# Opening stage of an encoder block regrouped by feature block, with keys, values and first queries accumulated together

## The chip, the core and the metric

The kernel runs on one NeuronCore of a Trainium2 chip. The metric is the device time of one execution in microseconds (us). Before the change it is 852.07 us, the median of 3 runs (851.49 to 852.62). One further execution was taken with the hardware profiler; every duration below comes from that one.

## What is computed

One layer of a bidirectional encoder on x (512 tokens, 1024 features, fp32). Cut to what matters here:

```python
mod = silu(c) @ w_ada + b_ada                 # (6 * 1024): shift1, scale1, gate1, shift2, scale2, gate2
h = rms_norm(x, norm1_gain) * (1 + scale1) + shift1
cb, cc, cu, q, k, v, ga, gb = split(h @ w_in) # 3x1024, 1024, 256, 256, 2x1024 columns
y_a = cb * dwconv3(cc * cu)
y_b = windowed_gqa(rms_norm(q), rms_norm(k), v, sink)   # 16 query heads, 4 key heads of 64
x = x + gate1 * ((sigmoid(ga) * y_a + sigmoid(gb) * y_b) @ w_o)
x = x + gate2 * conv_ffn(rms_norm(x) * (1 + scale2) + shift2)
```

## The kernel before

The program is written engine by engine, every wait by hand. A 128-feature slice of the 1024 features is a **block**; there are KT = 8. Each product of fp32 values is split: a value is rounded to a high part in fp32r (ScalarE, function `high`, line 480) and the rest is its low part (GpSimd, function `low`, line 404), and a product is three matmuls, high x high, high x low, low x high (`three`, lines 728 to 730). A **unit** is 128 output columns of a weight matrix times the 512 tokens: 8 blocks x 3 matmuls of 512 columns. Weights come as pairs of units (256 columns, 1 MB) through two slots `w_raw`.

The opening makes h and from it keys, values and the first queries:

- SyncE (SP) issues all loads in one queue: c, x (4 x 512 KB), the first two sixths of w_ada (shift1 and scale1) as 16 chunks of 512 KB, each the 128 rows of one k and 512 of the 1024 columns of both parts (line 342), small parameters after the fourth, and the key and value weights (line 314).
- VectorE (DVE) multiplies each chunk by silu(c) of its 128 rows and adds it to `acc0` (`gemv0`, line 1092), 1024 elements a partition at a time; chunk 8 is multiplied by TensorE instead (line 752). After chunks 0 to 7 the sum for blocks 0 to 3 is complete, after 8 to 15 that for blocks 4 to 7. Each half is transposed by TensorE (line 761), reduced (line 1099) and made into a shift `mod` and a factor `amp` (lines 1105, 1106).
- GpSimd (POOL) multiplies the transposed x by its row factors (`hT`, line 422). ScalarE (ACT) makes the high part of h (line 516), DVE its float value (line 1118), DVE or POOL its low part `h_lo` (lines 1123, 427).
- TensorE (PE) makes keys and values token by token, `token_major`, lines 728 to 730 with 256 columns: keys for blocks 0 to 3, values in part, then blocks 4 to 7. Only behind it stand the two query units, 48 matmuls of 512 columns. Keys are normalised on DVE (1144 to 1147), transposed (803), and split (534, 1163).

After the opening come, for each of the 4 groups g of heads, 10 or 12 units (kinds C, U, B, A, Q, G) in **slots** of half a unit (12 matmuls), between which the attention of the group stands at slots given by tables (`SCORE`, `TURN`, `Q0_TURN`). The first unit of group 0 (C) needs `q_st`, the split queries (line 1175). Then follow the output projection and the channel-mixing layer.

```python
for n in range(KT):
    gemv0(n)
mods(0)
```

are DVE's lines for the first half of the modulation; `mods(0)` waits for PE's `mod_turn(0)`.

## Time and profile before

| what | value |
|---|---|
| median of 3 runs | 852.07 us (851.49 to 852.62) |
| profiled execution, its own time | 850.04 us |
| its span, first to last instruction | 848.24 us |
| mean granted TensorE clock | 0.974 of full |
| PE busy | 793.4 us (94%) |
| DVE, ACT, POOL busy | 551.9, 366.7, 370.4 us |
| data read | 93.43 MB |

A span is read from its first instruction at 0. Durations of pipelined matmuls overlap: the distance between two starts is what one costs, the printed duration is longer. "Idle before" is the time in which the engine had nothing to do, with what ended it behind the arrow.

### The profile page before, as it was taken

To read this page: it belongs to the slowest core of one execution; us is meant where nothing else is said; L and a number is where in the kernel's file an instruction comes from. 1 tells how busy PE (TensorE), PEld (TensorE's weight loads), DVE (VectorE), ACT (ScalarE), POOL (GpSimd) and SP (SyncE) were. 2 spreads that over 40 slices of the span, in tenths; PEclk is the share of its full clock that TensorE was granted. 3 is DMA by queue.
4 is the path that set the end of the run, shared out by engine and by line. 5 is a ranking of instruction groups with operands and counts; after the bars stand their busy time and mean duration, and the time that the engine had idled before them with its cause. 6 is when DMAs were issued, how large, how long until landed. Compare 5 with 4: busy or idle time off the path is not lost.

```text
span 848.2 us, 10386 instructions
## 1 busy us (share of the span) xinstructions
PE 793.4 (94%) x3753; PEld 655.5 (77%) x3753; DVE 551.9 (65%) x710; ACT 366.7 (43%) x643; POOL 370.4 (44%) x169
## 2 busy tenths in 40 slices
PE   3579889999999999998999899999999999999997
PEld 2468768778788878886888788888888888887886
DVE  5978586767766776597735788888888888000000
ACT  6316355654565456545532534444444443112220
POOL 4825323433443333422853345555555554444340
PEclk9679999999999999999999899999999999999999
DMA  8913253143524352434233132222222332323311
GB/s 315 334 50 100 100 173 125 51 149 100 173 75 150 100 178 71 149 111 162 74 100 100 50 99 94 89 88 92 88 95 98 99 99 87 100 87 112 124 43 44
DMA packets 79740, 95.98 MB, mean 113 GB/s; under 512 B 2210, under 2 KB 71002, under 8 KB 79706
## 3 DMA queue, kind: packets, MB, share of 16 engines
q1 hardware_dynamic: 75482, 93.43, 33.0%
q10 hardware_dynamic: 4224, 2.10, 0.9%
q8 instruction: 21, 0.34, 0.2%
q14 instruction: 13, 0.11, 0.0%
HBM read 93.43 MB, written 2.10 MB: 113 GB/s over the span
## 4 chain that ended last, share of the span: by engine, by line
PE 71%; DVE 18%; ACT 4%; issue 4%; DMA 1%; SPq 1%; DVEq 0%; ACTq 0%
PE bank L728 22%; PE bank L729 22%; PE bank L730 22%; DVE acc L1212 4%; DVE sm L1235 2%; DVE prob L1228 1%; DVE acc L1092 1%; DVE a_buf L1273 1%; PE bank L894 1%; PE bank L868 1%; DVE pt_lo L1249 1%; DVE k_st L1163 1%; ACT prob L568 1%; PE bank L879 1%; DMA w_raw<-in_ffn_conv_b_dram 1%
## 5 line engine op out<-in xcount | busy, mean ns | idle before, releaser
L404 POOL TENSOR_TENSOR w_lo<-w_raw,w_hi 128x1024 fp32r<-128x1024 f32 x127 | 326.1, 2581 | 418.4 <-ACT w_hi L480 418.4
L728 PE MATMUL bank<-h_hi,w_hi 128*128 128x512 f32 (+1 forms) x792 | 308.3, 389 | 8.4 <-DVE h_lo L1405 3.6
L729 PE MATMUL bank<-h_lo,w_hi 128*128 128x512 f32 (+1 forms) x792 | 305.9, 386 | 0.0
L730 PE MATMUL bank<-h_hi,w_lo 128*128 128x512 f32 (+1 forms) x792 | 305.5, 386 | 0.0
L728 PEld LDWEIGHTS bank<-h_hi,w_hi 128*128 128x128 f32 x792 | 150.4, 190 | 39.4 <-issue 5.2
L480 ACT ACTIVATE w_hi<-w_raw 128x1024 fp32r<-128x1024 f32 x128 | 130.7, 1053 | 115.6 <-PE bank L730 107.2
L730 PEld LDWEIGHTS bank<-h_hi,w_lo 128*128 128x128 f32 x792 | 150.4, 190 | 29.8
L729 PEld LDWEIGHTS bank<-h_lo,w_hi 128*128 128x128 f32 x792 | 150.6, 190 | 28.6
L728 PE MATMUL bank<-g_hi,w_hi 128*128 128x512 f32 x176 | 70.0, 398 | 0.0
L729 PE MATMUL bank<-g_lo,w_hi 128*128 128x512 f32 x176 | 69.7, 396 | 0.0
L730 PE MATMUL bank<-g_hi,w_lo 128*128 128x512 f32 x176 | 69.5, 395 | 0.0
L1212 DVE SCALAR_TENSOR_TENSOR acc<-ada,c_act,acc 128x1024 f32<-128x1024 f32 x28 | 54.6, 1948 | 0.4
L582 ACT ACTIVATE pt_hi<-bank 128x512 fp32r<-128x512 f32 x40 | 22.1, 594 | 64.4 <-PE bank L879 64.4
L1228 DVE SCALAR_TENSOR_TENSOR prob<-bank,sm,bias 128x256 f32<-128x256 f32 (+1 forms) x64 | 32.0, 541 | 22.8 <-PE bank L868 22.8
L683 ACT ACTIVATE pad_f<-bank 128x512 f32<-128x512 f32 x22 | 13.1, 599 | 71.0 <-PE bank L730 71.0
L1468 DVE SCALAR_TENSOR_TENSOR y_buf<-bank,mod,xT 128x512 f32<-128x512 f32 x4 | 3.0, 751 | 60.3 <-PE bank L730 60.3
L568 ACT ACTIVATE prob<-prob,sm 128x256 f32<-128x256 f32 (+1 forms) x64 | 35.1, 554 | 16.3 <-DVE sm L1238 16.3
L1460 DVE TENSOR_TENSOR g_lo<-y_buf,g_hi 128x512 f32 x22 | 39.7, 1803 | 2.7
L1442 DVE SCALAR_TENSOR_TENSOR a_buf<-pad_f,par,a_buf 128x512 f32<-128x512 f32 x22 | 37.6, 1709 | 3.3 <-DVE a_buf L1440 1.7
L728 PEld LDWEIGHTS bank<-g_hi,w_hi 128*128 128x128 f32 x176 | 33.1, 188 | 8.0
L730 PEld LDWEIGHTS bank<-g_hi,w_lo 128*128 128x128 f32 x176 | 33.0, 188 | 7.9
L729 PEld LDWEIGHTS bank<-g_lo,w_hi 128*128 128x128 f32 x176 | 33.1, 188 | 7.8
(172 smaller groups left out, 990.9 us busy)
## 6 DMA issues: line engine op xcount, KB each, us to landing
w_raw<-in_w_in_dram SPq DMA_DIRECT2D x26, 1024.0 KB, 5.1
ada<-in_w_ada_dram SPq DMA_DIRECT2D x48, 512.0 KB, 6.1
w_raw<-in_w_up_dram SPq DMA_DIRECT2D x22, 1024.0 KB, 5.1
w_raw<-in_w_down_dram SPq DMA_DIRECT2D x8, 1024.0 KB, 5.0
w_raw<-in_w_o_dram SPq DMA_DIRECT2D x4, 1024.0 KB, 5.0
w_raw<-in_w_down_dram SPq DMA_DIRECT2D x4, 768.0 KB, 4.3
x_nat<-in_x_dram SPq DMA_DIRECT2D x4, 512.0 KB, 5.0
out_dram<-b_buf ACTq DMA_DIRECT2D x4, 256.0 KB, 2.3
```

The source lines that it names most:

```text
L404: pool.tensor_tensor(w_lo[:, n % 2, u], w_raw[:, n % 2, :, u * P:(u + 1) * P], w_hi[:, n % 2, u], SUB).then_inc(lo_ready, 1)
L480: act.activation(w_hi[:, n % 2, u], w_raw[:, n % 2, :, u * P:(u + 1) * P], ACT.Copy).then_inc(hi_ready, 1)
L568: act.activation(prob[:, b % 2, h, 0:w], prob[:, b % 2, h, 0:w], ACT.Exp, bias=sm[:, 1, b, h:h + 1], accum_out=sm[:, 3, b, h:h + 1]).then_ ...
L582: act.activation(pt_hi[:, t % 2, :], bank[TB[t % 2]][:, :], ACT.Copy).then_inc(pt_h, 1)
L728: pe.matmul(dst, w_h, rhs_hi, start=first, stop=False)
L729: pe.matmul(dst, w_h, rhs_lo, start=False, stop=False)
L730: return pe.matmul(dst, w_l, rhs_hi, start=False, stop=last)
L1212: dve.scalar_tensor_tensor(acc[:, :], ada[:, k % 2, :], c_act[:, 0, k:k + 1], acc[:, :], MUL, ADD).then_inc(ada_done, 1)
L1228: dve.scalar_tensor_tensor(prob[:, b % 2, h, 0:w], bank[SC[h % 2]][:, 0:w], sm[:, 6, b, h:h + 1], bias[:, h, c0:c0 + w], MUL, ADD).then_in ...
L1235: steps.link(dve.tensor_reduce(sm[:, 0, b, :], prob[:, b % 2, :, 0:w], AX.X, MAX))
L1442: dve.scalar_tensor_tensor(a_buf[:, u, :], pad[u][:, 2:S + 2], w(PA_FW + 2 * FT), a_buf[:, u, :], MUL, ADD).then_inc(conv_done, 1)
L1460: dve.tensor_tensor(lo, y_buf[:, u, :], hi, SUB).then_inc(ffn_tiles, 1)
```

## The change

Everything is now done block by block, t = 0 to 7. The other stages keep their instructions.

- **Loads.** x, then all small parameters, then w_ada in four groups of two blocks: a group has 4 chunks, each with 256 rows and the 256 columns of its two blocks, of both parts, issued as two loads of 256 KB. Between the groups stand, for each block, its 128 rows of the key and value weights (256 KB) and of the first query weights (128 KB). A chunk from the third group on waits until DVE has used its slot; a key and value row block from the fifth on waits for POOL.
- **Modulation.** DVE takes 8 multiply-adds of 256 elements for each block (64 in all) in place of 16 of 1024 (one of them on PE), then reduces the two columns of the block and makes one factor. PE transposes 2 x 128 columns a block.
- **h.** ACT writes the high part, and the float value to PSUM bank 6; DVE makes all low parts.
- **PE.** For each block 6 query matmuls and 12 matmuls of 512 columns (keys and values of 128 tokens side by side), in six banks; the transposes of the next block's sum stand behind the first 9.
- **Splits of weights** by ACT and POOL are per block too: 512 key and value columns and 2 x 128 query columns.
- **Keys.** They are squared by ACT, normalised on DVE by 8 instructions from PSUM, and transposed in group 0 (`K_TURN`, slots 3 to 5, 16 transposes where 8 stood in the opening), with both halves of the partitions holding the head. The attention of group 0 starts two slots later and its last part stands where it stood.

The diff, cut to its core:

```diff
-    P_MIX = 2
+    P_MIX = 0
...
-        ada0 = sb("ada0", [P, RING, 2, D // 2], into=start)
-        acc0 = sb("acc0", [P, 2, 2, D // 2], into=start)
-        c_b = sb("c_b", [P, P], into=start)
+        ada0 = sb("ada0", [P, RING, 2, 2, PC], into=start)
+        acc0 = sb("acc0", [P, 2, 2, P], into=start)
+        kv_hi = sb("kv_hi", [P, KT, 2 * PC], f32r, into=start)
+        kv_lo = sb("kv_lo", [P, KT, 2 * PC], f32r, into=start)
...
+        kv_raw = [b_buf[:, 0, :], b_buf[:, 1, :], y_buf[:, 0, :], y_buf[:, 1, :]]
+        spare = prob[:, :, :, :].rearrange("p i h j -> p (i h j)")
+        k_sq = spare[:, 0:NB * PC]
+        k_n = spare[:, NB * PC:3 * NB * PC].rearrange("p (b j o d) -> p b j o d", b=NB, j=KV, o=2)
...
+        def kv_bank(b):
+            return bank[2 + b][:, :]
         def v_heads(b):
...
+            return bank[2 + b][:, PC:2 * PC].rearrange("p (j d) -> p j d", d=HD)
+        def in_slot(n):
+            return 16 * ((n + 1) // 2)
...
-        SCORE = [(3, 7, 12, 16), (0, 5, 10, 15), (0, 5, 10, 15), (0, 4, 8, 12)]
-        TURN = [(9, 13, 17, 21), (6, 11, 16, 21), (6, 11, 16, 21), (6, 10, 14, 17)]
+        SCORE = [(5, 9, 13, 16), (0, 5, 10, 15), (0, 5, 10, 15), (0, 4, 8, 12)]
+        TURN = [(11, 15, 18, 21), (6, 11, 16, 21), (6, 11, 16, 21), (6, 10, 14, 17)]
         Q_TURN = (19, 21)
-        Q0_TURN = (0, 2)
+        Q0_TURN = (1, 2)
+        K_TURN = {3: (0,), 4: (1, 2), 5: (3,)}
...
+            parameters()
+            def kvq(t):
+                if t >= 4:
+                    sp.wait_ge(kv_l, t - 3)
+                rows = slice(t * P, (t + 1) * P)
+                sp.dma_start(kv_raw[t % 4], w_in[0, rows, COL_K:COL_K + 2 * PC]).then_inc(kvq_in[t % 4], 16)
+                sp.dma_start(w_raw[:, 0, t, :], w_in[0, rows, COL_Q:COL_Q + PC]).then_inc(kvq_in[t % 4], 16)
+            def ada_tiles(i):
+                by_tile = w_ada[0, :, 0:2 * D].rearrange("(k p) (s n) -> p k s n", p=P, s=2)
+                for a in range(KT // 2):
+                    n = i * (KT // 2) + a
+                    if n >= RING:
+                        sp.wait_ge(gemv_done, KT * (2 * i - 3) + 2 * a + 2)
+                    for s in range(2):
+                        sp.dma_start(ada0[:, n % RING, :, s, :],
+                                     by_tile[:, 2 * a:2 * a + 2, s, i * PC:(i + 1) * PC]).then_inc(ada0_in[n % RING], 16)
+            ada_tiles(0)
+            kvq(0)
+            kvq(1)
+            for i in range(1, KT // 2):
+                ada_tiles(i)
+                kvq(2 * i)
+                kvq(2 * i + 1)
+            sp.wait_ge(par_t, 2)
...
+            def start_low(t):
+                pool.wait_ge(kv_h, t + 1)
+                pool.tensor_tensor(kv_lo[:, t, :], kv_raw[t % 4], kv_hi[:, t, :], SUB).then_inc(kv_l, 1)
+                pool.wait_ge(*((q0_h, t + 1) if t < KT - 1 else (hi_ready, 2)))
+                ins = pool.tensor_tensor(w_lo[:, 0, :, t, :], w_raw[:, 0, t, :].rearrange("p (u n) -> p u n", u=2),
+                                         w_hi[:, 0, :, t, :], SUB)
+                ins.then_inc(*((q0_l, 1) if t < KT - 1 else (lo_ready, 2)))
             pool.wait_ge(r_copy, 1)
...
+            pool.wait_ge(xt_done, KT)
+            for t in range(KT):
+                if t:
+                    pool.wait_ge(*((xt_out, t + 1) if t < 6 else (xt_dve, t - 5)))
+                    pool.tensor_tensor(hT[:, t, :], xT[:, t, :], a_buf[:, 0, :], MUL).then_inc(xr_pool, 1)
+                start_low(t)
+            low(None, 0, P_MIX + 1)
+            pool.wait_ge(kv_done, NB)
...
+            def start_high(t):
+                act.wait_ge(kvq_in[t % 4], 32 * (t // 4) + 32)
+                act.activation(kv_hi[:, t, :], kv_raw[t % 4], ACT.Copy).then_inc(kv_h, 1)
+                ins = act.activation(w_hi[:, 0, :, t, :], w_raw[:, 0, t, :].rearrange("p (u n) -> p u n", u=2), ACT.Copy)
+                ins.then_inc(*((q0_h, 1) if t < KT - 1 else (hi_ready, 2)))
+            def h_high(t):
+                act.wait_ge(amp_done, t + 1)
+                act.wait_ge(*((xr_pool, t) if t else (xr_dve, 1)))
+                act.activation(h_hi[:, t, :], hT[:, t, :], ACT.Identity, bias=mod[:, t:t + 1],
+                               scale=amp[:, 0, t:t + 1]).then_inc(h_h, 1)
+                if t:
+                    act.wait_ge(h_ready, t)
+                act.activation(bank[OB][:, :], hT[:, t, :], ACT.Identity, bias=mod[:, t:t + 1],
+                               scale=amp[:, 0, t:t + 1]).then_inc(h_f, 1)
+            for m in range(4):
+                x_out(m)
+            act.wait_ge(xr_done, 1)
+            act.activation(a_buf[:, 0, :], bank[4][:, :], ACT.Copy).then_inc(r_copy, 1)
+            start_high(0)
             act.wait_ge(par_t, 2)
             for t, (r0, n) in enumerate(((0, ROWS1), (ROWS1, ROWS2))):
                 act.activation(par[:, r0:r0 + n], bank[5][:, (t + 1) * P:(t + 1) * P + n], ACT.Copy).then_inc(par_c, 1)
...
+            x_out(4)
+            x_out(5)
+            for t in range(KT):
+                if t == KT - 1:
                     high(None, 0, 1)
...
-            high(None, 0, P_MIX + 1)
...
+                h_high(t)
+                if t < KT - 1:
+                    start_high(t + 1)
...
+            def mod_turn(t):
+                pe.wait_ge(gemv_done, KT * (t + 1))
+                if t:
+                    pe.wait_ge(amp_done, t)
+                for s in range(2):
+                    mm = pe.transpose(bank[MB][:, s * P:(s + 1) * P], acc0[:, t % 2, s, :], ident[:, :])
+                mm.then_inc(red_done, 1)
+            mod_turn(0)
+            pe.wait_ge(xt_out, 6)
+            pe.wait_ge(xt_dve, 2)
             pe.wait_ge(par_c, 2)
...
+            for t in range(KT):
+                pe.wait_ge(h_ready, t + 1)
+                pe.wait_ge(*((q0_l, t + 1) if t < KT - 1 else (lo_ready, 2)))
+                for u in range(2):
+                    mm = three(bank[u][:, :], w_hi[:, 0, u, t, :], w_lo[:, 0, u, t, :], h_hi[:, t, :], h_lo[:, t, :],
+                               t == 0, t == KT - 1)
+                    if t == KT - 1:
+                        mm.then_inc(units_done, 1)
+                pe.wait_ge(kv_l, t + 1)
                 for b in range(NB):
...
+                    tokens = slice(b * P, (b + 1) * P)
+                    mm = three(kv_bank(b), h_hi[:, t, tokens], h_lo[:, t, tokens], kv_hi[:, t, :], kv_lo[:, t, :],
+                               t == 0, t == KT - 1)
+                    if t == KT - 1:
+                        mm.then_inc(kv_done, 1)
+                    elif b == 0:
+                        mod_turn(t + 1)
...
+            def key_turn(j):
+                if j == 0:
+                    pe.wait_ge(kn_ready, NB)
+                if j == 1:
+                    pe.wait_ge(m_free, 2)
+                if j >= 2:
+                    pe.wait_ge(kl_done, j - 1)
+                for b in range(NB):
+                    mm = pe.transpose(bank[OB + j % 2][:, b * P:(b + 1) * P],
+                                      k_n[:, b, j].rearrange("p o d -> p (o d)"), ident[:, :])
+                mm.then_inc(kt_done, 1)
...
+            def gemv0(t, ks):
+                for k in ks:
+                    n = (t // 2) * (KT // 2) + k // 2
+                    dve.wait_ge(ada0_in[n % RING], 32 * (n // RING) + 32)
+                    if k:
+                        dve.wait_ge(gemv_done, KT * t + k)
+                    dve.scalar_tensor_tensor(acc0[:, t % 2], ada0[:, n % RING, k % 2, :, (t % 2) * P:(t % 2 + 1) * P], c_act[:, 0, k:k + 1],
+                                             acc0[:, t % 2] if k else zero[:, :].unsqueeze(2).to_broadcast([P, 2, P]),
+                                             MUL, ADD).then_inc(gemv_done, 1)
+            def mods(t):
+                dve.wait_ge(red_done, t + 1)
+                dve.wait_ge(par_c, 2)
+                m2, b2 = (v.rearrange("p (s k) -> p s k", s=2)[:, :, t]
+                          for v in (mod[:, 0:2 * KT], par[:, PA_B:PA_B + 2 * KT]))
+                steps.link(dve.tensor_reduce(m2, bank[MB][:, 0:2 * P].rearrange("p (s n) -> p s n", n=P), AX.X, ADD))
+                steps.link(dve.tensor_tensor(m2, m2, b2, ADD))
+                dve.scalar_tensor_tensor(amp[:, 0, t:t + 1], mod[:, KT + t:KT + t + 1], 1.0,
+                                         par[:, PA_G1 + t:PA_G1 + t + 1], ADD, MUL).then_inc(amp_done, 1)
+            def h_low(t):
+                dve.wait_ge(h_f, t + 1)
+                dve.tensor_tensor(h_lo[:, t, :], bank[OB][:, :], h_hi[:, t, :], SUB).then_inc(h_ready, 1)
+            gemv0(0, range(HT))
...
+            gemv0(0, range(HT, KT))
+            dve.wait_ge(r_copy, 1)
+            dve.wait_ge(xt_out, 1)
+            dve.wait_ge(xt_done, KT)
+            dve.tensor_tensor(hT[:, 0, :], xT[:, 0, :], a_buf[:, 0, :], MUL).then_inc(xr_dve, 1)
+            for m in (6, 7):
+                dve.tensor_scalar(xT[:, m, :], bank[m % 4][:, :], 1.0, None, MUL).then_inc(xt_dve, 1)
+            for t in range(KT):
+                if t:
+                    gemv0(t, range(HT, KT))
+                mods(t)
+                if t < KT - 1:
+                    gemv0(t + 1, range(HT))
+                h_low(t)
...
+            for b in range(NB):
+                dve.wait_ge(kv_done, b + 1)
+                for o in range(2):
+                    dve.tensor_tensor(k_n[:, b, :, o], kv_bank(b)[:, 0:PC].rearrange("p (j d) -> p j d", d=HD),
+                                      st[:, 6, b * KV:(b + 1) * KV].unsqueeze(2).to_broadcast([P, KV, HD]),
+                                      MUL).then_inc((kn_half, kn_ready)[o], 1)
+            query_sums(0, 1)
+            for b in range(NB):
+                dve.wait_ge(v_high, b + 1)
+                dve.tensor_tensor(v_st[:, b, :, 1, :], v_heads(b), v_st[:, b, :, 0, :],
+                                  SUB).then_inc(score_free if b < 2 else t_free, 1)
+            query_norm(0)
+            def key_low(j):
+                dve.wait_ge(kh_done, j + 1)
+                dve.wait_ge(kq_done, 1)
+                dve.scalar_tensor_tensor(k_st[:, 1, j, :], bank[OB + j % 2][:, :], c_act[:, 1, 0:1], k_st[:, 0, j, :],
+                                         MUL, SUB).then_inc(kl_done, 1)
```

How the order of the instructions moves is shown at two engines. **DVE, modulation** (`acc0` the running sum, `ada0` the loaded chunk, `mod` and `amp` shift and factor, bank7 and bank4/5 the transposed sum). Before, in the first half:

```order
L1092 SCALAR_TENSOR_TENSOR acc0<-ada0,c_act,acc0 128x1024 [waits gemv_done,ada0_in4]
L1092 SCALAR_TENSOR_TENSOR acc0<-ada0,c_act,acc0 128x1024 [waits gemv_done,ada0_in5]
L1092 SCALAR_TENSOR_TENSOR acc0<-ada0,c_act,acc0 128x1024 [waits gemv_done,ada0_in6]
L1092 SCALAR_TENSOR_TENSOR acc0<-ada0,c_act,acc0 128x1024 [waits gemv_done,ada0_in7]
L1099 TENSOR_REDUCE mod<-bank4 128x4 [waits mod_summed]
L1099 TENSOR_REDUCE mod<-bank5 128x4 [waits mod_summed]
L1105 TENSOR_TENSOR mod<-mod,par 128x2x4 [waits par_copied,dve_steps]
L1106 SCALAR_TENSOR_TENSOR amp<-mod,par 128x4 [waits dve_steps]
```

Of the change, from the end of block 0 to the end of block 1:

```order
L1124 TENSOR_REDUCE mod<-bank7 128x2 [waits par_copied,mod_reduced]
L1125 TENSOR_TENSOR mod<-mod,par 128x2 [waits dve_steps]
L1126 SCALAR_TENSOR_TENSOR amp<-mod,par 128x1 [waits dve_steps]
L1114 SCALAR_TENSOR_TENSOR acc0<-ada0,c_act,zero 128x256 [waits ada0_in0]
L1114 SCALAR_TENSOR_TENSOR acc0<-ada0,c_act,acc0 128x256 [waits gemv_done,ada0_in0]
L1114 SCALAR_TENSOR_TENSOR acc0<-ada0,c_act,acc0 128x256 [waits gemv_done,ada0_in1] x2
L1131 TENSOR_TENSOR h_lo<-bank6,h_hi 128x512 [waits h_float]
L1114 SCALAR_TENSOR_TENSOR acc0<-ada0,c_act,acc0 128x256 [waits gemv_done,ada0_in2] x2
L1114 SCALAR_TENSOR_TENSOR acc0<-ada0,c_act,acc0 128x256 [waits gemv_done,ada0_in3] x2
L1124 TENSOR_REDUCE mod<-bank7 128x2 [waits par_copied,mod_reduced]
L1125 TENSOR_TENSOR mod<-mod,par 128x2 [waits dve_steps]
L1126 SCALAR_TENSOR_TENSOR amp<-mod,par 128x1 [waits dve_steps]
```

The instructions are a quarter as long, and the low part of h of a block (from bank6) stands behind the first four of the next block's. **PE, first products** (bank0 and bank1 queries, bank2 to bank5 keys and values). Before:

```order
L761 MATMUL bank4<-ident,acc0 128x128 [waits x_rstd_copied,gemv_done,par_copied]
L761 MATMUL bank4<-ident,acc0 128x128 x3
L761 MATMUL bank5<-ident,acc0 128x128 x4
L752 MATMUL bank6<-ada0,c_b 128x512 [waits ada0_in0,c_spread]
L752 MATMUL bank7<-ada0,c_b 128x512
L728 MATMUL bank0<-w_hi,h_hi 128x256 [waits h_ready,lo_ready]
L729 MATMUL bank0<-w_lo,h_hi 128x256
```

Of the change, in block 0:

```order
L771 MATMUL bank1<-h_hi,w_lo 128x512
L769 MATMUL bank2<-kv_hi,h_hi 128x512 [waits kv_low]
L770 MATMUL bank2<-kv_lo,h_hi 128x512
L771 MATMUL bank2<-kv_hi,h_lo 128x512
L800 MATMUL bank7<-ident,acc0 128x128 [waits amp_done,gemv_done]
L800 MATMUL bank7<-ident,acc0 128x128
L769 MATMUL bank3<-kv_hi,h_hi 128x512
L770 MATMUL bank3<-kv_lo,h_hi 128x512
L771 MATMUL bank3<-kv_hi,h_lo 128x512
L769 MATMUL bank4<-kv_hi,h_hi 128x512
```

The transposes of block 1's sum (bank7) stand between the first and the second batch of tokens.

## Rows read from the trace of the kernel before

**Rows 1.** Waits of PE in 0 to 100 us: us in total, times, longest.

```profile
PE bank L728 <- POOL w_lo L404: 3.5, 1, 3.5
PE bank L728 <- DVE q_st L1175: 3.5, 1, 3.5
```

**Rows 2.** Busy time by stretch: us and (instructions) of each engine, PEclk, DMA share, GB/s.

```profile
0.00:35.40 35.40, 12.19 (x50) 8.63 (x50) 24.81 (x32) 17.42 (x30) 20.30 (x19) 0.81 0.95 338
35.40:87.80 52.40, 42.18 (x260) 38.68 (x260) 43.02 (x48) 22.30 (x37) 26.52 (x15) 0.87 0.29 95
```

**Rows 3.** Timeline of PE: start us, us, instruction, [idle before <- releaser].

```profile
9.41 3.60 PE L741 MATMUL bank<-ident,x_nat 128*128 128x128 f32 x16 [6.78 <-DMA x_nat<-in_x_dram]
...
35.38 0.36 PE L728 MATMUL bank<-w_hi,h_hi 128*128 128x256 f32 x1 [1.91 <-DVE h_lo L1123]
...
73.03 0.40 PE L729 MATMUL bank<-h_lo,w_hi 128*128 128x512 f32 x1
73.26 0.40 PE L730 MATMUL bank<-h_hi,w_lo 128*128 128x512 f32 x1
...
83.73 0.60 PE L818 MATMUL bank<-ident,merged 128*128 128x128 f32 x4
87.84 0.68 PE L728 MATMUL bank<-h_hi,w_hi 128*128 128x512 f32 x1 [3.51 <-DVE q_st L1175]
88.32 0.63 PE L729 MATMUL bank<-h_lo,w_hi 128*128 128x512 f32 x1
88.75 0.63 PE L730 MATMUL bank<-h_hi,w_lo 128*128 128x512 f32 x1
```

**Rows 4.** One stretch with all engines while the opening loads (columns of rows 2).

```profile
20.00:25.00 5.00, 0.00 (x0) 0.00 (x0) 4.79 (x3) 0.00 (x0) 5.00 (x4) 0.50 1.08 366
```

**Rows 5.** Timeline of DVE, the opening (columns of rows 3).

```profile
10.48 0.17 DVE L1050 TENSOR_SCALAR st<-st 128x4 f32<-128x4 f32 x1 [6.73 <-ACT hT L493]
```

**Rows 6.** Timeline of POOL, the opening.

```profile
14.67 15.73 POOL L422 TENSOR_TENSOR hT<-xT,b_buf 128x512 f32<-128x512 f32 x8 [10.34 <-ACT b_buf L508]
30.36 2.33 POOL L404 TENSOR_TENSOR w_lo<-w_raw,w_hi 128x1024 fp32r<-128x1024 f32 x1
...
37.27 2.73 POOL L427 TENSOR_TENSOR h_lo<-y_buf,h_hi 128x512 fp32r<-128x512 f32 x2
39.97 6.65 POOL L404 TENSOR_TENSOR w_lo<-w_raw,w_hi 128x1024 fp32r<-128x1024 f32 x2
```

**Rows 7.** DVE groups by form: xcount | busy us, mean ns | idle before.

```profile
L1405 DVE SCALAR_TENSOR_TENSOR h_lo<-b_buf,mod,h_hi 128x256 fp32r<-128x256 f32 x6 | 2.9, 475 | 0.2 <-ACT h_hi L660 0.2
...
L1123 DVE TENSOR_TENSOR h_lo<-a_buf,h_hi 128x512 fp32r<-128x512 f32 x3 | 2.1, 686 | 0.0
...
L1382 DVE TENSOR_REDUCE st<-bank 128x2 f32<-128x256 f32 x2 | 0.9, 426 | 0.5 <-PE bank L966 0.5
```

**Rows 8.** Timeline of ACT, the opening (columns of rows 3).

```profile
55.05 2.93 ACT L516 ACTIVATE h_hi<-hT,mod,amp 128x512 fp32r<-128x512 f32 x4 [17.27 <-DVE amp L1106]
```

**Rows 9.** Timeline of DVE, four instructions in short windows.

```profile
13.39 1.28 DVE L1092 SCALAR_TENSOR_TENSOR acc<-ada,c_act,acc 128x1024 f32<-128x1024 f32 x1
...
14.79 2.23 DVE L1092 SCALAR_TENSOR_TENSOR acc<-ada,c_act,acc 128x1024 f32<-128x1024 f32 x1
...
30.85 1.87 DVE L1105 TENSOR_TENSOR mod<-mod,par 128x8 f32<-128x8 f32 x1
...
41.19 3.23 DVE L1092 SCALAR_TENSOR_TENSOR acc<-ada,c_act,acc 128x1024 f32<-128x1024 f32 x1
```

**Rows 10.** PE busy and granted clock by stretch, DMA share, GB/s.

```profile
33.30:36.70 3.40, 1.49 (x12) 1.00 1.05 386
36.70:40.00 3.30, 3.15 (x15) 0.50 1.03 344
84.00:87.80 3.80, 0.33 (x4) 1.00 0.00 0
87.80:91.30 3.50, 3.46 (x8) 0.52 0.26 67
```

302 lines of the change are left out of this document (68 added, 234 removed).

## Prediction

> **What bounds the kernel now.** I read the waits of TensorE first. In the first 100 us two of its longest waits are for GpSimd's low weights and for the split queries, 3.5 us each [rows 1]. Then the stretches: to 35.4 us TensorE has 12.19 us of work, to 87.8 us it has 42.18 of 52.40 [rows 2]; behind that it is busy nearly throughout, and the page gives 94% for the span. So only the opening can gain or lose, and what counts is when the first unit of group 0 (C) starts: at 87.84, behind 3.51 us of waiting for `q_st` [rows 3]. The opening's products start at 35.38 [rows 3], because half of the modulation must be summed first. The change lets them start behind an eighth of it, but hangs each next block on VectorE.
>
> Products are the same in columns: 192 of 256 and 48 of 512 before, 96 and 48 of 512 now. 144 x 0.23 us (73.03 to 73.26) is 33 us warm; cold the distance is 0.43 (88.32 to 88.75) [rows 3]. TensorE is not the scarce engine of this stretch.
>
> **First product, step by step.** x has landed at 9.41 [rows 3]. Two chunks of 0.52 MB behind it take 1.4 us each at 366 GB/s [rows 4]: 12.3. VectorE now does four multiply-adds ahead of the row factors of x, two of them behind the second chunk: it starts those at about 13.4, not at 10.48 [rows 5]. From there to the copied factors it was 4.2 us (GpSimd begins at 14.67 [rows 6]): 17.6. TensorE's last 12 transposes of x stand behind the spreading matmul, at 3.60/16 = 0.22 us each when cold [rows 3], then those of the parameters and of the sum: about 20.5. VectorE's normed block 0 and two copies, 0.7 us each (a 512-column instruction took 0.686 [rows 7]): 21.9. Reduction 0.43 [rows 7], two small ones of 0.17 and gaps, 0.9 together: 22.8. ScalarE's two passes, 0.7 each (four in 2.93 [rows 8]), lie beside four multiply-adds (2.1) and one hold by GpSimd (0.9, below): 25.8. Low part 0.69: the first product at **26.5, 8.9 us earlier**.
>
> **One block.** VectorE per block: 8 multiply-adds of 256. No row shows one; the nearest is L1405 with the same operands in form, 475 ns [rows 7]. Bounds are 0.43 (the reduction of 256) and 0.69 (512 columns) [rows 7]; I take 0.475 and 0.04 for the step to the next, since the form is the same: 4.1 us. Modulation 0.9, low part 0.7 with its gap: 5.7. The sum's transposes stand between the last multiply-add and the reduction, 0.45 with the signals: 6.15.
>
> Then GpSimd. The 1024-element multiply-add took 1.28 us alone and 3.23 beside GpSimd's `w_lo` of 1024, so 1.95 was waiting; beside `hT` of 512 it took 2.23, so 0.95 [rows 9]. An 8-element addition started at 30.85 and took 1.87 [rows 9]; GpSimd's instruction ran from 30.36 for 2.33 [rows 6], and both end at 32.7. So VectorE stands still for most of a GpSimd instruction, however short its own. Per block GpSimd now has two of 512 (0.9 each) and one of 256 (0.4 on the line between 0.95 and 1.95): 2.2 us. Where VectorE reads PSUM or waits for TensorE it costs nothing; that covers one half microsecond. On the path 1.7. **Block: 7.85 us; seven of them 55.0.** Bounds: 6.15 if all is covered, 8.35 if nothing is.
>
> The Trainium skill (SBUF — State Buffer, "Who interferes with whom") says the shared pair of ports is an exclusive lock that GpSimd has for the full instruction and that a VectorE instruction with two SBUF inputs fully blocks on it. By that rule, VectorE's waits agree with the rows in kind and are longer in length; what it would make of the time is the third rival.
>
> **Clock.** Of such a block TensorE has 4.1 us of products and pauses in two pieces. Before, the stretch 33.3 to 36.7 with 1.49 us busy was followed by one at clock 0.50, and 3.5 us idle by one at 0.52 [rows 10]. So some blocks will run cold. A cold block has 9 products (3.9 us instead of 2.1) and the transposes ahead of the reduction, where VectorE needs 3.0: it is 1.1 us longer. I take three of eight: 3.3. The last block's 18 products, warm: 4.1. C can start at 26.5 + 55.0 + 3.3 + 4.1 = **88.9, which is 1.1 us later** than 87.84.
>
> **What else moves.** C no longer waits for `q_st`: 12 products of keys and values stand behind the queries and cover ScalarE's split and VectorE's. Its first 8 products ran cold (3.46 us for 8 [rows 10]) and should now be warm: 8 x 0.20 = 1.6 less. The 16 key transposes cost 4 x 0.5 (four took 0.60 with the tail [rows 3]): 2.0 more; the 8 they replace were in the opening. Late next are the keys: squares, sums, eight normalising instructions (0.42 each at least) reach about 9.0 us behind C, slot 3 comes at 9.2, so the cover is 0.2 us; behind that, the second pair of key transposes waits for VectorE's low part. I take 0.5, between 0 and 3. Group 0's attention starts two slots later and ends in the same slot: 0, with 2 either way, since its waits shift. Unit U's weights are asked for when block 7's are split, some 5 us before C, and needed 13 us behind C: 0. The queue moves the same 13.6 MB in the opening; at 366 GB/s that is 37 us, the two reused groups are asked for a block or more ahead of use: 0, and if GpSimd or VectorE hold them up the block's own length already says so. The small parameters move ahead of the chunks: 11 issues, behind the 2 MB of x: 0.
>
> **Sum.** +1.1 - 1.6 + 2.0 + 0.5 = **+2.0 us**. The profiled execution took 850.04 (span 848.24 and 1.8 around it): 852.0 for it. The median of the runs is 2.0 above that execution, so I say **854.1**. A measurement of this kernel can tell 0.2%, 1.7 us, from no change; +2.0 is just outside.
>
> **Rivals.**
> - *GpSimd's holds fall beside VectorE's PSUM reads (faster).* A block has 1.6 us in which VectorE needs no shared port (low part, reduction, transposes). If the holds settle there, only 0.8 of the 2.2 is on the path: 7 x 0.9 = 6.3 less, and one cold block fewer, 1.1. That is -5.4: 846.7. It decides from 1.4 us a block on. For it: GpSimd's work is triggered by ScalarE right behind h, where the low part stands. Against: `hT` and `w_lo` follow one another into the next multiply-adds. Chance 0.27.
> - *TensorE stays cold in most blocks (slower).* Six of eight, the last too: 3 x 1.1 + 18 x 0.20 = 6.9 more: 861.0. For it: every block has pauses. Against: a cold block is nearly full (18 x 0.43 of 8.9) and a full stretch was followed by a warm one. Chance 0.14.
> - *GpSimd holds the port for its whole instruction (slower).* Alone one of 512 takes 1.37 (two in 2.73), one of 1024 2.33 [rows 6], so one of 256 about 0.9: 3.6 a block instead of 2.2, 10 us in seven blocks: 864. The two contended ones of 1024 took 3.3 each (6.65 [rows 6]), and VectorE waited 1.95 of that, which speaks against it. Chance 0.05, in which I count a late load too. It is the length that the Trainium skill's page (SBUF — State Buffer) gives.
> - *Errors cancel to nothing.* 852.1, within 1.7: chance 0.04.
>
> **Chances.** My forecast has 0.50 and its own range 850 to 858 (block 7.3 to 8.3 us): 0.06 of it faster, 0.17 same, 0.27 slower. The first rival is faster but for 0.02. With the others: faster 0.06 + 0.25 = 0.31, same 0.17 + 0.02 + 0.04 = 0.23, slower 0.27 + 0.14 + 0.05 = 0.46. The range reaches to the rivals on both sides: 845.5 to 861.
>
> **What would show it.** First product near 26.5; starts of two blocks' first query products 7.3 to 8.5 apart, the multiply-adds 0.47 alone and 0.9 to 1.4 behind GpSimd; some blocks at clock 0.5; no wait on loads; C at 88 to 90 with no wait on `q_st`; in group 0 a short wait ahead of key transposes. I am wrong if the multiply-adds do not lengthen beside GpSimd (then blocks of 6.2 and C near 77), if TensorE waits for loads, or if a wait in group 0 exceeds 3 us.

## The result and the profile after

The changed kernel takes **856.36 us** (median of 5 runs, 854.88 to 860.26) where the kernel before takes 851.76 beside it (848.86 to 852.62, 5 runs): a ratio of 1.0072, with a 95% interval of 1.004 to 1.0103. It is slower by more than the 0.2% that a measurement can tell. The profiled execution took 854.88 us (span 853.1) against 850.04 (span 848.24), 4.84 more. Single executions of 2777 to 2779 us (one of the kernel before and one each of two kernels below) are left out of the ratios.

The waits of TensorE in the first 110 us, the view of [rows 1]:

```profile
PE bank L769 <- DVE h_lo L1131: 15.8, 7, 6.4
PE bank L800 <- DVE acc L1114: 11.9, 6, 4.5
...
PE bank L850 <- DVE prob L1210: 2.3, 1, 2.3
```

The waits for GpSimd's low weights and for the split queries [rows 1] are gone. In their place TensorE waits twice in every block for VectorE: for the low part of h, and for the sum of the modulation. TensorE waits for no load of weights.

The stretches to the first product, to C, and one of five whole blocks between (columns of [rows 2]):

```profile
0.00:28.10 28.10, 10.11 (x39) 7.94 (x40) 13.94 (x36) 14.82 (x28) 6.72 (x14) 0.94 0.85 291
28.10:90.70 62.60, 41.21 (x158) 29.58 (x158) 49.43 (x82) 20.73 (x34) 27.75 (x22) 0.94 0.43 139
36.00:76.00 40.00, 24.69 (x101) 17.24 (x102) 33.87 (x61) 12.47 (x21) 18.12 (x16) 1.00 0.34 112
```

In 36 to 76 us TensorE is busy for 62% and its granted clock stays at 1.00, 2.4 GHz. Timeline of TensorE, the view of [rows 3]: first product, second block, seventh and eighth (which is the last), C and the first key transposes.

```profile
28.12 0.76 PE L769 MATMUL bank<-h_hi,w_hi 128*128 128x512 f32 x1 [6.39 <-DVE h_lo L1131]
...
35.95 0.50 PE L769 MATMUL bank<-h_hi,w_hi 128*128 128x512 f32 x1 [1.58 <-DVE h_lo L1131]
39.77 0.44 PE L800 MATMUL bank<-ident,acc 128*128 128x128 f32 x2 [1.47 <-DVE acc L1114]
...
75.70 0.50 PE L769 MATMUL bank<-h_hi,w_hi 128*128 128x512 f32 x1 [1.57 <-DVE h_lo L1131]
...
82.52 0.46 PE L800 MATMUL bank<-ident,acc 128*128 128x128 f32 x2 [4.47 <-DVE acc L1114]
...
86.44 0.39 PE L769 MATMUL bank<-h_hi,w_hi 128*128 128x512 f32 x1
...
90.75 0.47 PE L769 MATMUL bank<-h_hi,w_hi 128*128 128x512 f32 x1
...
102.48 0.66 PE L850 MATMUL bank<-ident,prob 128*128 128x128 f32 x4 [2.25 <-DVE prob L1210]
```

The first product starts at 28.12, 7.3 us earlier than the 35.38 of [rows 3]. The first products of the blocks then stand 7.83 to 7.97 us apart, but the last interval (75.70 to 86.44) is 10.74. C starts at 90.75, 2.9 later than the 87.84 of [rows 3]. Behind C, 4.2 more go in group 0, as the first instruction that writes `merged` of a group shows (the sum of the two gated branches; below it is called the first `merged` and serves as the marker for the end of group 0). Here it is of groups 0 and 3 in the changed kernel:

```profile
183.13 0.69 DVE L1303 SCALAR_TENSOR_TENSOR merged<-b_buf,a_buf 128x512 f32<-128x512 f32 x1
...
421.38 1.66 DVE L1303 SCALAR_TENSOR_TENSOR merged<-b_buf,a_buf 128x512 f32<-128x512 f32 x1
```

and in the kernel before:

```profile
176.00 0.69 DVE L1292 SCALAR_TENSOR_TENSOR merged<-b_buf,a_buf 128x512 f32<-128x512 f32 x1
...
415.92 1.66 DVE L1292 SCALAR_TENSOR_TENSOR merged<-b_buf,a_buf 128x512 f32<-128x512 f32 x1
```

The distance is 7.13 behind group 0, 7.15 and 7.12 behind the next two, 5.46 behind group 3 and 4.86 at the end. So 2.3 us come back late: 1.7 between the markers of groups 2 and 3, where the kernel before ran a stretch at the lower clock and this execution did not, and 0.6 behind the marker of group 3, for which I have no cause.

**A block on three engines.** VectorE, GpSimd and ScalarE of the changed kernel around one amplitude (`amp`): VectorE's and GpSimd's work ahead of it, then VectorE's and ScalarE's behind it.

```profile
43.74 3.93 DVE L1114 SCALAR_TENSOR_TENSOR acc<-ada,c_act,acc 128x256 f32<-128x256 f32 x4
48.21 0.43 DVE L1124 TENSOR_REDUCE mod<-bank 128x2 f32<-128x256 f32 x1 [0.53 <-PE bank L800]
...
48.87 0.16 DVE L1126 SCALAR_TENSOR_TENSOR amp<-mod,par 128x1 f32<-128x1 f32 x1
48.94 0.48 DVE L1114 SCALAR_TENSOR_TENSOR acc<-ada,c_act,zero 128x256 f32<-128x256 f32 x1
49.52 1.66 DVE L1114 SCALAR_TENSOR_TENSOR acc<-ada,c_act,acc 128x256 f32<-128x256 f32 x3
51.11 0.68 DVE L1131 TENSOR_TENSOR h_lo<-bank,h_hi 128x512 fp32r<-128x512 f32 x1
```

```profile
43.22 1.28 POOL L438 TENSOR_TENSOR kv_lo<-y_buf,kv_hi 128x512 fp32r<-128x512 f32 x1 [4.37 <-ACT kv_hi L531]
44.45 0.92 POOL L440 TENSOR_TENSOR w_lo<-w_raw,w_hi 128x256 fp32r<-128x256 f32 x1
45.34 1.46 POOL L449 TENSOR_TENSOR x_nat<-xT,a_buf 128x512 f32<-128x512 f32 x1
```

```profile
49.06 0.81 ACT L539 ACTIVATE h_hi<-x_nat,mod,amp 128x512 fp32r<-128x512 f32 x1 [5.61 <-DVE amp L1126]
49.78 0.76 ACT L543 ACTIVATE bank<-x_nat,mod,amp 128x512 f32<-128x512 f32 x1
50.49 0.61 ACT L531 ACTIVATE kv_hi<-b_buf 128x512 fp32r<-128x512 f32 x1
```

(`x_nat` is the memory that now also holds `hT`.) Four multiply-adds without GpSimd take 2.24 us from the start of the first to the end of the last (48.94 to 51.18), where 2.1 was forecast; the four beside GpSimd's three instructions take 3.93, so 1.7 of it is waiting. Seen one by one, the first three of these end at 44.77, 45.66 and 47.08, each 0.3 us behind one of GpSimd's (44.50, 45.37, 46.80): in this row one gets through per GpSimd instruction. The fourth takes 0.48 and ends at 47.67, 0.87 behind GpSimd's last. What that distance means was found only late in the runs below.

**The last block.** VectorE and GpSimd at the end of the opening:

```profile
75.56 6.90 DVE L1114 SCALAR_TENSOR_TENSOR acc<-ada,c_act,acc 128x256 f32<-128x256 f32 x4
83.02 0.43 DVE L1124 TENSOR_REDUCE mod<-bank 128x2 f32<-128x256 f32 x1 [0.56 <-PE bank L800]
```

```profile
75.04 1.28 POOL L438 TENSOR_TENSOR kv_lo<-y_buf,kv_hi 128x512 fp32r<-128x512 f32 x1 [4.38 <-ACT kv_hi L531]
76.28 0.93 POOL L440 TENSOR_TENSOR w_lo<-w_raw,w_hi 128x256 fp32r<-128x256 f32 x1
77.17 5.02 POOL L420 TENSOR_TENSOR w_lo<-w_raw,w_hi 128x1024 fp32r<-128x1024 f32 x2
```

ScalarE splits C's weights ahead of the last h, so GpSimd's two low parts of 1024 stand beside the last multiply-adds of the modulation, on which everything hangs.

**The key chain.** VectorE behind the queries, with GpSimd below:

```profile
92.49 1.21 DVE L1203 TENSOR_REDUCE st<-prob 128x16 f32<-128x1024 f32 x1
93.73 1.81 DVE L1084 TENSOR_SCALAR st<-st 128x16 f32<-128x16 f32 x1
...
96.63 0.24 DVE L1089 RECIPROCAL st<-st 128x16 f32<-128x16 f32 x1
96.90 2.33 DVE L1090 SCALAR_TENSOR_TENSOR st<-st 128x16 f32<-128x16 f32 x1
```

```profile
93.12 2.40 POOL L420 TENSOR_TENSOR w_lo<-w_raw,w_hi 128x1024 fp32r<-128x1024 f32 x1
96.82 2.38 POOL L420 TENSOR_TENSOR w_lo<-w_raw,w_hi 128x1024 fp32r<-128x1024 f32 x1 [1.31 <-ACT w_hi L500]
```

Two instructions of 16 elements take 1.81 and 2.33 us, where one takes 0.17 without GpSimd (99.27): they end with GpSimd's (95.52 and 99.20). The eight normalising ones come that much later, and TensorE waits 2.25 at its key transposes.

### The profile page after: what moved, and what is told of

The parts are those of the page before. It is cut to its first block, busy times and chain, and to the rows that moved or that the text cites. A ratio compares the mean times of both kernels' runs of the same rounds, so it can differ in the third digit from the quotient of the medians.

```text
span 853.1 us, 10374 instructions
## 1 busy us (share of the span) xinstructions
PE 789.7 (93%) x3661; PEld 645.7 (76%) x3661; DVE 557.4 (65%) x772; ACT 370.0 (43%) x655; POOL 363.7 (43%) x176
## 4 chain that ended last, share of the span: by engine, by line
PE 72%; DVE 20%; ACT 4%; issue 3%; SPq 1%; DMA 1%; DVEq 0%
PE bank L769 22%; PE bank L770 22%; PE bank L771 22%; DVE acc L1114 5%; DVE acc L1196 3%; PE bank L897 1%; PE bank L925 1%; DVE a_buf L1284 1%; DVE sm L1246 1%; DVE prob L1239 1%; PE bank L908 1%; DVE pt_lo L1260 1%; ACT prob L608 1%; DVE h_lo L1415 1%; DVE pad_f L1276 1%
## 5 line engine op out<-in xcount | busy, mean ns | idle before, releaser
L420 POOL TENSOR_TENSOR w_lo<-w_raw,w_hi 128x1024 fp32r<-128x1024 f32 x122 | 312.2, 2572 | 401.9 <-ACT w_hi L500 401.9
L500 ACT ACTIVATE w_hi<-w_raw 128x1024 fp32r<-128x1024 f32 x122 | 124.7, 1052 | 106.3 <-PE bank L771 106.2
L1196 DVE SCALAR_TENSOR_TENSOR acc<-ada,c_act,acc 128x1024 f32<-128x1024 f32 x28 | 48.8, 1743 | 0.4
L1114 DVE SCALAR_TENSOR_TENSOR acc<-ada,c_act,acc 128x256 f32<-128x256 f32 x56 | 41.8, 746 | 5.2 <-DMA ada<-in_w_ada_dram 0.3
```

Source lines behind the costliest of these rows:

```text
L420: pool.tensor_tensor(w_lo[:, n % 2, u], w_raw[:, n % 2, :, u * P:(u + 1) * P], w_hi[:, n % 2, u], SUB).then_inc(lo_ready, 1)
L500: act.activation(w_hi[:, n % 2, u], w_raw[:, n % 2, :, u * P:(u + 1) * P], ACT.Copy).then_inc(hi_ready, 1)
L1114: dve.scalar_tensor_tensor(acc0[:, t % 2], ada0[:, n % RING, k % 2, :, (t % 2) * P:(t % 2 + 1) * P], c_act[:, 0, k:k + 1], acc0[:, t % 2] ...
L1196: dve.scalar_tensor_tensor(acc[:, :], ada[:, k % 2, :], c_act[:, 0, k:k + 1], acc[:, :], MUL, ADD).then_inc(ada_done, 1)
```

## The experiments

Ratios are to the kernel before on the same chip. Where a kernel had one timed run only, its trace is what it was made for. "C" is the start of unit C's first product. C and the first `merged` are read from one execution of each kernel.

**Theory:** VectorE waits for GpSimd, in the blocks, in the last block and in the key chain. **Rivals:** TensorE's turn or clock, loads, or VectorE's own work.

### C's weights split late

```diff
             for t in range(KT):
-                if t == KT - 1:
-                    high(None, 0, 1)
                 h_high(t)
                 if t < KT - 1:
                     start_high(t + 1)
+            high(None, 0, 1)
```

> ScalarE splits C's weights behind both passes of block 7 instead of ahead of them, so GpSimd's two low parts of C (5.02 us from 77.17) come behind VectorE's last eight multiply-adds. Theory (VectorE stands still beside GpSimd): the four multiply-adds ahead of block 7's reduction take about 2.1 to 2.3 us instead of 6.90, the last interval between first products falls from 10.74 to 6.0 to 8.0 us, the window 82.7 to 86.2 is no longer cold, and C starts 2 to 4 us earlier, at 87 to 88.8, unless it waits up to 1 us for its own low weights; the kernel 2 to 3 us shorter than the changed one. Rival (the last block is long for its load or for TensorE's turn): the interval stays within 0.5 us of 10.74. Rival (the wait only moves: C's low weights come too late): interval near 8, but a wait of 2 us or more on the low weights ahead of C and no gain.

The last interval is 6.62 us (76.49 to 83.11), the clock stays at 1.00 (79.5 to 87.5), C at 87.58 without a wait, 3.2 earlier; ratio 1.0047 (1.0025 to 1.007) where the changed kernel had 1.0072 (1.004 to 1.0103): the two intervals overlap, so the gain is shown by the trace and only made likely by the times. VectorE's four multiply-adds:

```profile
76.36 3.10 DVE L1113 SCALAR_TENSOR_TENSOR acc<-ada,c_act,acc 128x256 f32<-128x256 f32 x4
```

That is 3.10 and not the 2.1 to 2.3 expected, since the block's own two instructions of GpSimd are still beside them. The interval is what the theory said and both rivals fall: 3.8 of the 6.90 us were C's weights.

### U's second half late

```diff
-            high(None, 0, 2, (1,))
             for b in range(NB):
                 act.wait_ge(kn_ready, b + 1)
                 act.activation(v_st[:, b, :, 0, :], v_heads(b), ACT.Copy).then_inc(v_high, 1)
+            high(None, 0, 2, (1,))
```

> ScalarE splits the second half of U's weights behind the four value copies, so GpSimd's low part of it (2.38 us from 96.82) no longer stands in the key chain. Theory: the small instruction that began at 96.90 takes 0.2 us instead of 2.33, the normalised keys are ready 1.8 to 2.3 us earlier, the wait of 2.25 us ahead of the first key transposes is gone or under 0.5, the eight products behind it run at 0.23 us instead of 0.43 and so 1.6 us less: 3.5 to 4 us less up to the end of that stretch, 2 to 4 us less in the kernel. Rival (the keys are late for VectorE's own reduction and eight normalising instructions): the wait stays over 1.5 us. Rival (the price is given back): the wait goes, but later waits in group 0 (low part of U's weights, values behind the heads) grow and the first merged of group 0 stays within 1 us of 183.1.

A miss, and the most useful one: 1.0088 (1.0073 to 1.0103), slower than the kernel before and not faster than the changed kernel, from whose 1.0072 the times cannot tell it. The small instruction takes 0.18, the keys are ready in time, and the wait ahead of the first transposes is gone. But TensorE and VectorE then show

```profile
106.78 0.66 PE L850 MATMUL bank<-ident,prob 128*128 128x128 f32 x4 [3.31 <-DVE k_st L1224]
129.12 1.51 PE L897 MATMUL bank<-k_st,q_st 128*128 128x384 f32 x4 [2.81 <-DVE prob L1239]
```

```profile
101.88 1.55 DVE L1090 SCALAR_TENSOR_TENSOR st<-st 128x16 f32<-128x16 f32 x1
103.46 2.26 DVE L1091 TENSOR_TENSOR st<-st 128x16 f32<-128x16 f32 x1
...
109.80 2.81 DVE L1190 TENSOR_SCALAR acc<-ada,c_act 128x1024 f32<-128x1024 f32 x1 [0.86 <-DMA ada<-in_w_ada_dram]
...
124.94 3.50 DVE L1196 SCALAR_TENSOR_TENSOR acc<-ada,c_act,acc 128x1024 f32<-128x1024 f32 x1
```

GpSimd's instruction met the query norms instead (two small ones, 1.55 and 2.26), and two whole-width instructions of group 0 now stood beside GpSimd: 2.81 instead of 0.75, 3.50 instead of 1.28. The last rival is right in kind and too mild: the first `merged` comes at 185.29, 2.2 later than 183.13. Taking this wait out only moved it.

### Row factors of x first

```diff
-            gemv0(0, range(HT))
             dve.wait_ge(x_sq, NB)
...
-            gemv0(0, range(HT, KT))
+            gemv0(0, range(KT))
             dve.wait_ge(r_copy, 1)
```

> VectorE makes the row factors of x and their diagonals ahead of the first four multiply-adds instead of behind them. Theory (the four multiply-adds with their two waits for the chunks, 11.99 to 14.37, sit in the chain of the row factors): the spreading matmul comes 2.5 to 3.6 us earlier than 16.63, the first product at 24.5 to 26.5 instead of 28.12, all blocks as long as before, and the kernel 1.5 to 3.5 us shorter. Rival (the last chunks or TensorE's transposes hold the start): the first product stays within 0.5 us of 28.1. Rival (the blocks catch up on loads): the first product is earlier, but a block waits for keys' and values' weights and C starts no earlier.

First product at 25.29, 2.83 earlier, as the theory has it; C only 1.80 earlier, at 88.95. The first `merged` is 1.92 later (185.05): the scores of block 1 wait 3.15 us for VectorE, whose multiply-add ahead of them took 3.50 beside GpSimd instead of 1.28. Ratio 1.0043 (1.0023 to 1.0063).

This run also tells how far one execution can be trusted. Behind the start its code is the changed kernel's, yet from C to the first `merged` it takes 96.10 us where the changed kernel takes 92.38. Its eleven times form two groups, six from 850.66 to 853.54 and five from 855.96 to 856.91, and the profiled one (856.79) is of the second. So a difference of some 3 us between two kernels in that marker can come from where a few instructions happen to meet, and not from the edit.

### Without GpSimd's low parts

```diff
-                pool.tensor_tensor(kv_lo[:, t, :], kv_raw[t % 4], kv_hi[:, t, :], SUB).then_inc(kv_l, 1)
...
-                    mm = three(kv_bank(b), h_hi[:, t, tokens], h_lo[:, t, tokens], kv_hi[:, t, :], kv_lo[:, t, :],
+                    mm = three(kv_bank(b), h_hi[:, t, tokens], h_lo[:, t, tokens], kv_hi[:, t, :], kv_hi[:, t, :],
```

and the same for the query weights of blocks 0 to 6. The loads that waited for GpSimd's low part now wait for ScalarE's high part.

> Leaves out GpSimd's low parts of the keys', values' and first queries' weights in blocks 0 to 6 and the keys' and values' one in block 7; TensorE takes the high parts in their place, so it has as many products. Per block GpSimd keeps one instruction of 512. Theory (VectorE waits 1.67 us a block for the shared port): the four multiply-adds behind h's low part take about 3.0 us or less instead of 3.91, blocks of 6.5 to 7.2 us instead of 7.93 to 7.96, C 5 to 9 us earlier. Rival (TensorE's turn, its clock, or the loads set the block): blocks stay within 0.2 us of 7.94. Rival (the waits come from the number of instructions, not from GpSimd): the same.

```profile
42.36 0.50 PE L768 MATMUL bank<-h_hi,w_hi 128*128 128x512 f32 x1 [1.57 <-DVE h_lo L1130]
...
49.18 0.50 PE L768 MATMUL bank<-h_hi,w_hi 128*128 128x512 f32 x1 [1.58 <-DVE h_lo L1130]
```

Blocks of 6.82, the four multiply-adds in 2.80, C at 84.33, 6.4 earlier (0.6 of it in the start). TensorE has as many products and VectorE the same work, so GpSimd's two instructions cost 1.1 us a block. The time, 850.75, is one run; the kernel leaves out more than half of GpSimd's work in the blocks.

### The low part of keys and values twice

```diff
+                for n in range(2):
+                    if n:
+                        pool.wait_ge(kv_l, 2 * t + 1)
                     pool.tensor_tensor(kv_lo[:, t, :], kv_raw[t % 4], kv_hi[:, t, :], SUB).then_inc(kv_l, 1)
```

> The mirror of the run that left GpSimd's low parts out: GpSimd writes each block's low part of the keys' and values' weights twice (the same values), one more instruction of 512 per block and nothing else. Theory (VectorE stands still beside GpSimd, about 0.9 us per instruction of 512): the four multiply-adds behind h's low part take 4.6 to 5.0 us instead of 3.91, blocks are 8.6 to 9.0 us instead of 7.94, C starts 5 to 7 us later than 90.75. Rival (GpSimd's length does not matter to VectorE, or its later part is covered by PSUM reads): blocks stay within 0.2 us of 7.94.

Blocks of 8.75 to 8.97 behind a first one of 8.28, four multiply-adds in 4.72, C at 98.68, 7.9 later (3.4 of it in the start: first product at 31.53); 864.40 in one run. Within its bounds but for the first block and C. Together with the run before: GpSimd's work beside VectorE's sets the block, and TensorE, its clock and the loads do not.

### Query norms behind the keys

```diff
-            query_norm(0)
...
                             key_low(j)
+                    if g == 0 and slot == 4:
+                        query_norm(0)
```

> On the kernel with C's weights split late: VectorE makes the query norms behind the second and third low parts of the keys instead of ahead of the first. In the run without this edit the last small instruction of the norms began at 102.55 and took 2.22 beside GpSimd, the first low part of the keys began at 104.81, and TensorE waited 1.90 at 105.61. Theory (that small instruction stood in the chain of the keys): the wait of 1.90 falls under 0.5, the first merged comes 1 to 2 us earlier than 180.52. Rival (the wait only changes its place: ScalarE's splitting or the first scores are late instead): the first merged stays within 0.5 us of 180.52, with a new wait on the queries' norms or the scores' factors.

This run and the next stand on the kernel with C's weights split late, so they are compared with that one. The wait of 1.90 is gone, and the first `merged` is at 181.89, **1.4 later** than 180.52, though C was 1.9 earlier in this run (85.70). VectorE's whole-width instructions took 2.77 and 3.50 beside GpSimd and the scores of block 1 waited 2.65 (0.94 without the edit). The rival had the wait moving, but no loss; and a difference of this size lies within what one execution can show by chance. One run, 853.84.

### Both halves of U together

```diff
             high(None, 0, 2, (0,))
-            root(None, 0, 1, NB * KV, 1, 2)
             high(None, 0, 2, (1,))
+            root(None, 0, 1, NB * KV, 1, 2)
```

> On the kernel with C's weights split late: ScalarE splits both halves of U's weights together ahead of the root of the keys' norms. Theory: GpSimd's two low parts of U run back to back from 90.5 and end near 95.5, so the small instruction that took 2.33 at 94.28 waits 1.0 to 1.3 us only, the 2.25 us ahead of the first key transposes become about 1.0 to 1.3, and the first merged comes 1.0 to 1.5 us earlier than 180.52 (2.5 if the eight products behind the shorter wait are warm where they were cold). Rival (a small instruction waits for whole GpSimd instructions, one after the other): both small instructions now wait 2.3 us, and the keys come no earlier.

The small instruction waits 0.97 instead of 2.33 and the wait at the key transposes is 0.87 instead of 2.25, as the theory says. From C to the first `merged` it is 93.20 us against 92.94 in the run without this edit, so nothing reached the end of group 0; the 1.5 us that its `merged` is earlier (179.03) come from the start. The wait of 1.90 behind it is still there. One run, 852.28.

### All of it together

Besides the edits above (U's halves together, not late), one line for a multiply-add of 1024 in group 0:

```diff
+                    if g == 0 and slot == 9:
+                        gemv(g, GEMV_AT[3])
...
-                    if kind and slot // 2 - 1 in GEMV_AT:
+                    if kind and slot // 2 - 1 in GEMV_AT and (g, slot) != (0, 8):
```

> All edits that should take VectorE's waits beside GpSimd off the path: C's weights split late, row factors of x first, both halves of U's weights split together, query norms behind the keys' low parts, and in group 0 one multiply-add of 1024 behind the first scores of block 1 instead of ahead of them. Theory: C starts 5 to 5.5 us earlier than 90.75, waits ahead of the key transposes sum to 1.5 us or less, the wait at the scores of block 1 is under 1 us, first merged at 173 to 177 against 183.13, and the kernel takes 843 to 849 in a chip on which the kernel before takes 851: faster than before by 2 to 7 us. Rival (group 0 gives it back, as it did in the runs with the early start and with the late half of U): C earlier by 5, but first merged not under 178, and the kernel within 2 us of the kernel before.

**847.55 us**, ratio 0.9976 (0.9961 to 0.999): 0.2% faster than the kernel before, at the edge of what can be told. C at 83.52, 7.2 earlier where 5 to 5.5 was expected; from C to the first `merged` 90.07 (changed kernel 92.38, before 88.16). With the multiply-add behind the scores, the wait at block 1's scores is gone (none over 0.4 us); one of 0.96 for a turned low part stands behind it. That edit did not run alone, but the runs above agree: where the multiply-add ahead of `take` took 1.28 the scores waited 0.94, where it took 3.50 they waited 2.65, 2.81 and 3.15.

### The turn of the sum

```diff
+                if t < KT - 1:
+                    gemv0(t + 1, (0,))
                 mods(t)
                 if t < KT - 1:
-                    gemv0(t + 1, range(HT))
+                    gemv0(t + 1, range(1, HT))
```

> On the tuned kernel (all five edits): VectorE does the next block's first multiply-add (0.48 us) ahead of the reduction, while TensorE turns the finished sum, instead of behind it. In every block VectorE waited 0.53 us there, the 0.45 of my prediction's block. Theory (the turn is on the path and the multiply-add fits beside it): blocks of 7.5 to 7.75 us instead of 7.94, C starts 1.3 to 3 us earlier than 83.52. Rival (the path leaves VectorE there and runs over ScalarE's two passes to the low part, which three multiply-adds no longer cover): VectorE waits the same 0.4 to 0.5 us ahead of the low part, blocks stay within 0.1 us of 7.94.

On the tuned kernel. The multiply-add fits beside the turn and VectorE waits only 0.13 there, yet blocks stay at 7.93 to 7.96 and C comes 0.45 earlier (83.07), not 1.3 to 3: what it gained it now waits for in the next four.

```profile
47.52 4.43 DVE L1113 SCALAR_TENSOR_TENSOR acc<-ada,c_act,acc 128x256 f32<-128x256 f32 x4
51.87 0.48 DVE L1113 SCALAR_TENSOR_TENSOR acc<-ada,c_act,zero 128x256 f32<-128x256 f32 x1
```

```profile
49.63 1.45 POOL L449 TENSOR_TENSOR x_nat<-xT,a_buf 128x512 f32<-128x512 f32 x1
```

GpSimd ends at 51.08 and the four at 51.95, 0.87 behind it, the same distance as in the changed kernel. Neither the theory nor the rival: VectorE had slack, and the block is a **ring**: amplitude; ScalarE's two passes and its split (2.07 from 49.03 to 51.10); GpSimd's three instructions, 0.1 later (3.58); VectorE's last multiply-adds (0.87); turn (0.53); reduction and amplitude (0.8). The sum is 7.95. The two earlier runs fit. With the low part twice, GpSimd's four instructions take 4.97, VectorE's last multiply-add ends 0.28 behind them, and the ring gives 8.76 where blocks are 8.75 to 8.77. Without the low parts, GpSimd's one instruction ends 2.05 ahead of the four multiply-adds (49.79 against 51.85), so there the ring does not bind and VectorE's own work gives the 6.82. Ratio 0.9954 (0.9939 to 0.997) against 0.9976 of the tuned kernel; the intervals overlap.

### Other slots in group 0

```diff
-        SCORE = [(5, 9, 13, 16),
+        SCORE = [(5, 9, 12, 16),
-        TURN = [(11, 15, 18, 21),
+        TURN = [(11, 14, 17, 21),
```

> On the tuned kernel: in group 0 the scores of block 2 go from slot 13 to 12, the turns of blocks 1 and 2 from slots 15 and 18 to 14 and 17. Theory (the two waits for the heads of the block before, 1.71 at 154.71 and 1.66 at 168.34, come because the change's tables leave three slots between turns where the other groups have five): both fall under 0.5, group 0 is 1.5 to 3.4 us shorter, first merged at 170.2 to 172 against 173.59. Rival (the waits are GpSimd's or VectorE's doing whatever the slots): they stay over 1.2 each, or move to the scores or to the turned low parts, and merged stays within 0.7 us of 173.59.

No gain: 0.9971 (0.9955 to 0.9987), and the first `merged` at 175.37 instead of 173.59, outside what theory and rival allowed. The two waits for the heads become one of 2.03, and one of 1.75 ahead of the next group's scores comes back, like the 1.70 that the kernel before has there. Together with the turn's edit and one more multiplication moved behind the scores:

> The tuned kernel with both edits of this batch, and in group 0 also the first whole-width multiplication (2.84 us at 101.37, of which 0.75 is its own) behind the first scores instead of ahead of them. Theory: the parts add up: C near 81 to 82.2, first merged at 167 to 170, the kernel 4 to 6 us shorter than the tuned one: 841.5 to 844 where the kernel before takes 850. Rival (each later edit only moves a wait): no more than 2 us shorter than the tuned one.

0.9976 (0.9961 to 0.9992), 848.88, with C at 83.36 and the first `merged` at 173.87: the parts do not add up, and the rival holds.

### GpSimd's x out of the ring

```diff
                     pool.wait_ge(*((xt_out, t + 1) if t < 6 else (xt_dve, t - 5)))
+                    pool.wait_ge(amp_done, t)
```

> On the tuned kernel with the early first multiply-add: GpSimd makes the next block's normed x behind the amplitude of the block before (while ScalarE makes h), so that only two of its three instructions follow ScalarE's split of the weights. Its work is the same in every block. Theory formed from the last run (the block is a ring: amplitude, ScalarE's two passes and a split 2.07, GpSimd's three instructions 3.58, VectorE's last two multiply-adds 0.88, turn 0.53, reduction and amplitude 0.8): with 1.45 us of GpSimd out of the ring blocks are 6.8 to 7.4 us instead of 7.95, C starts 3 to 6 us earlier than 83.07, and the kernel takes 840.5 to 844.5 where the one without the edit took 846.6. Rival (my prediction's sum: a block is VectorE's own work plus what GpSimd's instructions hold, wherever they lie): GpSimd holds as long as before, so blocks stay within 0.2 us of 7.95. Rival (the hold now delays h's low part, and TensorE with it): the low part comes 0.9 us later behind the amplitude, TensorE's wait ahead of the first product of a block grows to 2 us, and the block gains under 0.3.

On the tuned kernel with the turn's edit, whose ring stands above. VectorE, then GpSimd, in one block:

```profile
44.00 2.50 DVE L1114 SCALAR_TENSOR_TENSOR acc<-ada,c_act,acc 128x256 f32<-128x256 f32 x3
46.42 0.68 DVE L1131 TENSOR_TENSOR h_lo<-bank,h_hi 128x512 fp32r<-128x512 f32 x1
47.02 2.96 DVE L1114 SCALAR_TENSOR_TENSOR acc<-ada,c_act,acc 128x256 f32<-128x256 f32 x4
```

```profile
44.23 1.41 POOL L450 TENSOR_TENSOR x_nat<-xT,a_buf 128x512 f32<-128x512 f32 x1 [2.95 <-DVE amp L1126]
46.25 1.39 POOL L438 TENSOR_TENSOR kv_lo<-b_buf,kv_hi 128x512 fp32r<-128x512 f32 x1 [0.61 <-ACT kv_hi L532]
47.60 0.91 POOL L440 TENSOR_TENSOR w_lo<-w_raw,w_hi 128x256 fp32r<-128x256 f32 x1
```

Blocks of 7.24 instead of 7.95 by one added wait, with GpSimd's work unchanged; C at 79.83, first `merged` at 169.94. **843.38 us**, ratio **0.9947** (0.9927 to 0.9966): 0.5% faster than the kernel before on the same chip, and the lowest ratio here, though its interval overlaps that of the run without the added wait (0.9954). The rival that holds stay as they were wherever GpSimd's work lies falls. The last rival is there in part (TensorE's wait for h is 1.83), but the block gains 0.7. VectorE is now idle for 0.14 us in the block (50.37 to 50.51), so with the ring loosened its own work and some 1.5 of holds make up the 7.24.

## Why the prediction was right, and where it was wrong

The forecast of 854.1 lies 2.3 us under the measured median, and slower was the likeliest sign, with a chance of 0.46. VectorE's queue with GpSimd's holds was rightly named as what the blocks hang on. That the number came out near is in good part luck: the sum was +2.0 where the profiled executions differ by 4.84, and in it 3.3 for cold blocks that did not come about stood in for 2.9 that the last block took and the sum left out. Step by step:

- **First product, 26.5.** It is 28.12, and 26.75 to 28.46 in the four runs whose start is the same code. The step that was late here was "at about 13.4": the four multiply-adds with their wait for the second chunk ended at 14.37, and the amplitude took 1.18 behind GpSimd. +1.6. The six kernels with the row factors first start at 24.04 to 25.29, so this order costs between 1.5 and 4.4 us.
- **Block, 7.85.** Measured 7.93 to 7.97 in all but the first: +0.5 over six. The wait beside GpSimd is 1.7, as forecast. A multiply-add is 0.48, but 0.54 to 0.59 from one to the next where I had 0.515, so eight take 4.4 and not 4.1; the turn is 0.53 for 0.45, modulation and low part together 1.3 for 1.6. But the step "5.7 + 0.45 + 1.7", a sum of VectorE's work, was not what sets the block: the turn's edit freed 0.48 of it for nothing, and the added wait took 0.7 off with all of the work left. The ring sets it, and that both come to 7.9 is luck.
- **Cold blocks, 3.3.** None of five blocks between 36 and 76 us is cold, at 62% busy with two pauses of 1.5 us each. The stretch from 28 to 36 us was at 0.77 and cost nothing, for its interval was 7.83. Nine products of the seventh block, behind TensorE's wait of 4.47, did run cold (0.43 apart, 82.72 to 86.20), but h's next low part ended only at 86.08, so 0.3 us of that counts. −3.3. That argument came from two stretches of the kernel before [rows 10], one of which was followed by the lower clock at 44% busy; nothing there spoke for a share of 62%.
- **The last of the seven blocks.** "Seven of them 55.0" took it as long as the others. C's own low weights, of which my steps say nothing, stand in it: 6.90 instead of 3.93 for the four multiply-adds, interval 10.74 instead of 7.85. This is the largest term that the sum had at nothing: +2.9, shown by splitting them late. Their place in ScalarE's order stood in the code.
- Last block 4.3 for 4.1. Together 1.6 + 0.5 − 3.3 + 2.9 + 0.2 = 1.9: C at 90.75 and not 88.9.
- **Group 0: forecast +0.9 behind C.** From C to `merged` it is +4.2 (92.38 against 88.16). The first eight products were warm and the wait on `q_st` is gone, as said. "I take 0.5" for the keys was 2.25 and 0.33, as well as products at the lower clock behind it (0.66 in 104 to 108), and the scores of block 1 wait 0.94. The bound of 3 held, the value did not: I had counted the keys' instructions without their waits for GpSimd. The step "group 0's attention starts two slots later: 0" did not hold either: waits of 1.71 and 1.66 for the heads of the block before are new, where the kernel before has 1.88 ahead of scores and 1.6 for turned low parts. Together TensorE waits 6.9 us between C and `merged` and 3.5 in the kernel before, so 3.4 more where my sum had 0.5; that is most of the 3.3 that are missing. What each would give back alone is not shown; single edits only moved them, and the row-factor run shows that one execution can differ by 3 us here.
- **Late: −2.3.** Nothing in my steps. Both kernels have a wait of TensorE for a turned low part here (2.66 at 384.80 before, 2.72 at 391.85 now), but only before did products at the lower clock follow (clock 0.86 in 380 to 392, against 1.00 in 387 to 399 now). No run was made for it, and whether it is in most executions of either kernel stays open.

Of the rivals: GpSimd's holds did not settle beside PSUM reads (1.7 were on VectorE's queue, not 0.8), TensorE was cold in parts of the first and the seventh block only, and VectorE did not lose the whole length of GpSimd's instructions: 3.66 us of them cost it 1.7. The Trainium skill's "exclusive lock" (SBUF — State Buffer, "Who interferes with whom") is seen in the small instructions, which end with GpSimd's. In a row of multiply-adds one gets through behind each of GpSimd's. GpSimd's own instructions are then longer as well, 0.92 for 256 and 1.46 for 512 (44.45 and 45.34) where the first ones took 0.72 and 1.25 (23.15 and 23.83), as if the two took turns; that this is a handing over of the port is my reading and was not tested.

## What to carry to other kernels

When a step is repeated and several engines hand it on, follow one signal round once (here amplitude, split, low part, multiply-add, turn) and add what lies on it; the sum of the busiest engine's work can give the same number and the wrong edit. Before moving a whole-width GpSimd instruction, list what VectorE has queued in its span: a 16-element instruction on the chain of the bound pays as much as a long one (2.2 here, and 2.1 for a multiplication of 1024). A wait taken out is worth what the next marker shows, here the first `merged`, and not its own length, and one execution of each kernel is too few for that where the times form two groups.

## What the runs showed that I had not expected

- Not every VectorE instruction waits beside GpSimd. A reduction of 1024 from SBUF took 1.21 us beside GpSimd's `bias` and 1.22 beside `w_lo` (the kernel before, 65.50), as long as alone (1.22, the changed kernel at 189.38). A reciprocal of 16 elements took 0.24 beside GpSimd (101.61, with U's second half late) and 0.24 alone (104.47 in the changed kernel). Multiply-adds, additions of two tensors and multiplications by a scalar waited, the last up to 2.41 for 16 elements (90.51, with C's weights late).
- How much a few hundredths of a microsecond decide: the multiplication L1190 of 1024 ran from 110.33 to 111.08 and took 0.75, with GpSimd's next instruction at 111.14; in the run with U's second half late it began 0.13 behind GpSimd's (109.80 against 109.67) and took 2.81. The recorded starts do not tell all of it: in the same run the multiply-add at 124.94 stands 0.05 ahead of GpSimd's instruction (124.98) and took 3.50 all the same.
- A wait *added* on GpSimd shortened the opening: C comes at 79.83 instead of 83.07, and the first `merged` at 169.94 instead of 173.12, with every instruction kept. The two ratios, 0.9947 and 0.9954, were taken on different chips and overlap, so the 3.2 us are shown by the traces and not by the times.
